# Gate and up of a SwiGLU layer: two of eight row pairs as seven block products, and x and weights asked for in order of use

## The reference

```python
h = rms_norm(x, norm_mix); proj = h @ w_in
# three head groups: gated linear attention, mLSTM, and spatial gating, whose mask is
# w_causal = tril(sgu_w)
x = x + mix @ w_out
hf = rms_norm(x, norm_ffn)
gate, up = jnp.split(hf @ w_gu, 2, axis=-1)      # w_gu: 2048 x 11264
x = x + (silu(gate) * up) @ w_down               # w_down: 5632 x 2048
return rms_norm(x, norm_final)
```

## Time and profile before

| | |
|---|---|
| median of three runs | 1117.72 us (1117.01 to 1117.94) |
| profiled execution | 1117.11 us |
| its span, first to last instruction | 1115.4 us |
| busy in the span | PE 1102.0, DVE 728.7, ACT 544.9, POOL 41.6 us |
| mean granted TensorE clock | 0.996 |
| DMA | 211.10 MB, 189 GB/s |

### The profile page before, as it was taken

How to read it: one execution, slowest core, us unless ns; L and a number is a source line. 1 busy time by engine, 2 the same in 40 slices (tenths; PEclk the granted TensorE clock), 3 DMA queues, 4 the chain that set the end, 5 groups by cost and what they waited for, 6 DMA issues and landing times.

```text
span 1115.4 us, 14031 instructions
## 1 busy us (share of the span) xinstructions
PE 1102.0 (99%) x5157; PEld 921.0 (83%) x5157; DVE 728.7 (65%) x871; ACT 544.9 (49%) x653; POOL 41.6 (4%) x66
## 2 busy tenths in 40 slices
PE   8999999999999999999999999999999999999996
PEld 7898889888888888888888888888888888888885
DVE  5456867698656555555555645555555799898895
ACT  6455545555445453444444434434444556656553
POOL 2700000000010000000000000000000000000000
PEclk9999999999999999999999999999999999999999
DMA  8665646565556666666666666666666656666663
GB/s 278 208 200 170 182 131 181 152 171 155 184 198 206 183 187 194 188 186 198 185 197 186 185 195 187 182 195 188 189 186 188 206 192 212 202 200 208 202 220 112
DMA packets 110059, 211.10 MB, mean 189 GB/s; under 512 B 6844, under 2 KB 11008, under 8 KB 109632
## 3 DMA queue, kind: packets, MB, share of 16 engines
q1 hardware_dynamic: 108960, 205.75, 60.8%
q0 software_dynamic: 1056, 4.77, 1.2%
HBM read 208.40 MB, written 2.10 MB: 189 GB/s over the span
## 4 chain that ended last, share of the span: by engine, by line
PE 96%; DVE 2%; DMA 1%; ACT 0%; issue 0%; SPq 0%; POOL 0%; ACTq 0%; POOLq 0%; DVEq 0%
PE acc L1187 24%; PE acc L1188 24%; PE acc L1189 24%; PE acc L1472 5%; PE acc L1474 5%; PE acc L1473 5%; PE mx L1179 2%; PE mx L1472 1%; PE mx L1474 1%; PE mx L1473 1%; PE mx L1358 1%; PE mx L1264 1%; DMA tok<-in_x 1%; DVE w_lo L1061 1%; DVE x L1049 0%
## 5 line engine op out<-in xcount | busy, mean ns | idle before, releaser
L658 DVE TENSOR_TENSOR w_lo<-raw,w_hi 128x1024 fp32r<-128x1024 f32 (+2 forms) x304 | 362.4, 1198 | 326.4 <-ACT w_hi L399 326.2
L399 ACT ACTIVATE w_hi<-raw 128x1024 fp32r<-128x1024 f32 (+2 forms) x304 | 314.4, 1039 | 397.3 <-PE acc L1189 387.6
L1187 PE MATMUL acc<-w_hi,hT_hi 128*128 128x512 f32 (+2 forms) x1084 | 418.5, 386 | 0.0
L1188 PE MATMUL acc<-w_lo,hT_hi 128*128 128x512 f32 (+2 forms) x1084 | 415.3, 383 | 0.0
L1189 PE MATMUL acc<-w_hi,hT_lo 128*128 128x512 f32 (+2 forms) x1084 | 415.3, 383 | 0.0
L1189 PEld LDWEIGHTS acc<-w_hi,hT_lo 128*128 128x128 f32 x1084 | 203.5, 188 | 40.1
L1187 PEld LDWEIGHTS acc<-w_hi,hT_hi 128*128 128x128 f32 x1084 | 203.6, 188 | 39.6 <-ACT tok L424 0.4
L1188 PEld LDWEIGHTS acc<-w_lo,hT_hi 128*128 128x128 f32 x1084 | 203.6, 188 | 38.7
L600 ACT ACTIVATE w_hi<-raw 128x1024 fp32r<-128x1024 f32 x88 | 83.2, 969 | 34.3 <-PE acc L1474 17.9
L1061 DVE TENSOR_TENSOR w_lo<-raw,w_hi 128x1024 fp32r<-128x1024 f32 x88 | 94.5, 1111 | 7.8 <-ACT w_hi L600 5.7
L1474 PE MATMUL acc<-w_hi,actT_lo 128*128 128x512 f32 x250 | 97.3, 389 | 0.0
(11 more groups left out here) (245 smaller groups left out, 828.4 us busy)
## 6 DMA issues: line engine op xcount, KB each, us to landing
raw<-in_w_gu SPq DMA_DIRECT2D x176, 512.0 KB, 3.7
raw<-in_w_down SPq DMA_DIRECT2D x88, 512.0 KB, 4.4
raw<-in_w_in SPq DMA_DIRECT2D x80, 512.0 KB, 4.0
raw<-in_w_out SPq DMA_DIRECT2D x32, 512.0 KB, 4.0
raw<-in_w_in SPq DMA_DIRECT2D x8, 272.0 KB, 2.8
raw<-in_w_in SPq DMA_DIRECT2D x8, 264.0 KB, 2.8
tok<-in_x SPq DMA_DIRECT2D x8, 256.0 KB, 7.4
x<-in_x POOLq DMA_DIRECT2D x2, 1024.0 KB, 9.3
```

The lines of the kernel that those rows point to most:

```text
L399: act.activation(w_hi[:, slot, 0:UC * width], raw[:, slot, 0:UC * width], ACT.Copy)\
L658: dve.tensor_tensor(w_lo[:, slot, 0:UC * width], raw[:, slot, 0:UC * width], w_hi[:, slot, 0:UC * width].bitcast(F32), ALU.subtract).then_ ...
L1187: pe.matmul(o, hi[:, c + i, tb], wh, start=first and i == 0, stop=False)
L1188: pe.matmul(o, hi[:, c + i, tb], wl, start=False, stop=False)
```

## The change

Groups 1 to 10 of gate and up take row pairs 0 and 1 as sevens: the 2 x 2 weight block is here (row block) by (gate, up), so the loads for these pairs bring the gate and the up weights of the same rows. A group has 16 loads and 20 slots in a new order `FF_ORDER`: gate 2, gate 3, seven 0, gate 4, gate 5, seven 1, gate 6, gate 7, up 2 to up 7. Group 0 stays as it was (`first_gate_up`), and makes the sums of the normed x that the sevens need (`ff_summands`). The bank sums are folded in each group (`fold_up`, `fold_gate`, `activate_folded`). The transposes of `act_tok` now stand behind the group's first unit, since the sevens use the `mx` banks.

The sums and summands lie where `x1` lies. So `x1` is stored to device memory once it is complete and loaded back when gate and up are done; DVE waits for the store in `ff_summands` and for the load in `fold_banks`.

At the start the DMAs are issued as x quarter 0, units 0 and 1, quarter 1, units 2 and 3, quarters 2 and 3, unit 4. Two x steps go ahead of the first unit, the others one by one behind units 0 to 5; each is followed by the weights of one unit on ACT and DVE. Four warm matmuls are added ahead of the x transposes and five behind the first two steps. The squares of x move from behind units 5 and 6 to behind units 8 and 9.

```diff
+FF_ORDER = [("gate", 2, 0, 0), ("gate", 3, 1, 1), ("seven", 0, 2, 2), ("gate", 4, 4, 6), ("gate", 5, 5, 7),
+            ("seven", 1, 6, 8), ("gate", 6, 8, 12), ("gate", 7, 9, 13)] + [("up", k, 8 + k, 12 + k) for k in range(2, UPG)]
+FF_SLOTS = 20
+FF_BASE = U_FF + 2 * UPG - FF_SLOTS
+FF_SLOT_OF = [-4, -3, -2, -1] + [v + d for kind, _k, _i, v in FF_ORDER for d in ((0, 1) if kind == "seven" else (0,))]
+V_DN = FF_BASE + FF_SLOTS * NG_FF
...
-WARM = 8
+WARM, WARM_X, WARM_W = 8, 4, 5
+X_AHEAD = {0: (0,), 2: (1,), 4: (2, 3)}
 LAST = 3
-START_UNITS = [0, 1, 4, 5]
...
-            for q in range(4):
-                for b in range(NB):
-                    sp.dma_start(xin[:, b, q * GW:(q + 1) * GW],
-                                 x[b * P:(b + 1) * P, q * GW:(q + 1) * GW]).then_inc(sem(f"x_loaded{b}{q}"), 16)
-                c0, width, _at = IN_GROUPS[0]
-                load(w_in, q, q, q * UC * P, c0, width, first=True)
-            for u in range(R, U_OUT):
+            for u in range(U_OUT):
+                for q in X_AHEAD.get(u, ()):
+                    for b in range(NB):
+                        sp.dma_start(xin[:, b, q * GW:(q + 1) * GW],
+                                     x[b * P:(b + 1) * P, q * GW:(q + 1) * GW]).then_inc(sem(f"x_loaded{b}{q}"), 16)
                 c0, width, _at = IN_GROUPS[u // UPG]
-                load(w_in, u, u % R, (u % UPG) * UC * P, c0, width)
+                load(w_in, u, u % R, (u % UPG) * UC * P, c0, width, first=u < R)
...
+            def load_ff(j, k, i, up):
+                sp.wait_ge(lo_ready, j * FF_SLOTS + (FF_BASE + FF_SLOT_OF[i] + 1))
+                sp.dma_start(raw[:, i % R, :].rearrange("p (k n) -> p k n", k=UC),
+                             weights(w_gu, k * UC * P, j * GW + (FF if up else 0), GW)).then_inc(loaded[i % R], 16)
+
+            for j in range(1, NG_FF):
+                for kind, k, i, _v in FF_ORDER:
+                    if kind == "seven":
+                        load_ff(j, k, i, False)
+                        load_ff(j, k, i + 1, True)
+                    else:
+                        load_ff(j, k, i, kind == "up")
 
...
+            pool.wait_ge(sem("residual_added"), 2 * NG_OUT)
+            for b in range(NB):
+                pool.dma_start(x1_kept[b * P:(b + 1) * P, :], x1[:, b, :]).then_inc(sem("x1_stored"), 16)
+
+            pool.wait_ge(unit_used, V_DN)
+            pool.wait_ge(sem("gate_used"), 2 * NG_FF)
+            pool.wait_ge(sem("x1_stored"), 16 * NB)
+            for b in range(NB):
+                pool.dma_start(x1[:, b, :], x1_kept[b * P:(b + 1) * P, :]).then_inc(sem("x1_back"), 16)
...
-                if b in START_UNITS:
-                    k = START_UNITS.index(b)
-                    high(k, k, GW, 16, fresh=True)
-
-            for u in range(R, U_FF):
+                high(b, b % R, GW, 16 * (b // R + 1), fresh=b < R)
+
+            for u in range(UPG, U_FF):
                 g = u // UPG
                 high(u, u % R, IN_GROUPS[g][1] if g < NG_IN else GW, 16 * (u // R + 1))
                 if u % UPG == 3 and 1 <= g <= NG_IN:
                     evacuate(g - 1)
-                if u in (5, 6):
-                    b = u - 5
+                if u in (8, 9):
+                    b = u - 8
...
+            def gate_up(j):
+                for kind, k, i, v in FF_ORDER:
+                    if kind == "up" and k == 3:
+                        act.wait_ge(unit_used, j * FF_SLOTS + (FF_BASE + 12))
+                        act.activation(ff_sum[:, 0, 0, :], mx[:, 2, :], ACT.Copy).then_inc(sem("p1_kept"), 1)
+                    ff_high(j, i, v)
+                    if kind == "seven":
+                        ff_high(j, i + 1, v + 1, GW)
+                        ff_sum_high(j, 0, v + 2, 2 * k + 1)
+                        if k == 0:
+                            act_high(j, j * 4 - 4)
+                        ff_sum_high(j, 1, v + 3, 2 * k + 2)
+                    if kind == "up" and k == 5:
+                        act.wait_ge(sem("gate_folded"), j * 2)
+                        gate_tanh(j * FF_SLOTS + (FF_BASE + 14), j * 2)
+
+            first_gate_up()
             with act.Fori(1, NG_FF) as j:
-                gate_up(j, False)
+                gate_up(j)
 
...
+            def activate_folded(groups, used):
+
+                for b in range(NB):
+                    if b == 0:
+                        dve.wait_ge(sem("up_block0"), groups)
+                        dve.wait_ge(sem("up_folded"), groups * 2)
+                    else:
+                        dve.wait_ge(unit_used, used)
+                    dve.tensor_tensor(up_part(b), acc[:, 2 + b, :], up_part(b), ALU.add).then_inc(sem("up_whole"), 1)
+                    if b == 0:
+                        dve.wait_ge(sem("gate_used"), groups * 2 + 2)
+                        dve.wait_ge(sem("actT_psum"), groups)
+                    dve.wait_ge(sem("up_whole"), groups * 2 + (b - 1))
+                    dve.scalar_tensor_tensor(out=act_tok[:, b, :], in0=up_part(b), scalar=half_rs2_h[:, b:b + 1],
+                                             in1=gate_s[:, b, :], op0=ALU.mult, op1=ALU.mult)\
+                       .then_inc(sem("act_ready"), 1)
+
...
+            def ff_weight_sums(j, i, k, opening=False):
+
+                a = i % R
+                for slot in range(2):
+                    dve.wait_ge(loaded[a + slot], j * (16 * 2 * UPG // R) + 16 * ((U_FF + i) // R + 1))
+                if k == 1:
+                    dve.wait_ge(lo_ready, j * FF_SLOTS + (FF_BASE + 6))
+                elif opening:
+                    dve.wait_ge(sem("ff_lo_ready"), 1)
+                else:
+                    dve.wait_ge(sem("gate_folded"), j * 2 - 2)
+                dve.tensor_tensor(ff_sum[:, 0, :, :], raw[:, a + 1, :].rearrange("p (k n) -> p k n", k=UC),
+                                  raw[:, a:a + 2, 0:GW], ALU.subtract).then_inc(sem("ff_w_sums"), 1)
+                dve.wait_ge(sem("ff_w_sums"), j * 4 + (2 * k - 3))
+                dve.tensor_tensor(ff_sum[:, 1, 0, :], raw[:, a + 1, GW:2 * GW], ff_sum[:, 0, 0, :], ALU.subtract)\
+                   .then_inc(sem("ff_t2"), 1)
+                dve.wait_ge(sem("ff_t2"), j * 2 + (k - 1))
+                dve.tensor_tensor(ff_sum[:, 1, 1, :], raw[:, a, GW:2 * GW], ff_sum[:, 1, 0, :], ALU.subtract)\
+                   .then_inc(sem("ff_w_sums"), 1)
+
+            p1, t6, t7 = (ff_sum[:, i // 2, i % 2, :] for i in range(3))
+
+            def fold_up(j):
+
+                dve.wait_ge(unit_used, j * FF_SLOTS + (FF_BASE + 12))
+                dve.wait_ge(sem("p1_kept"), j)
+                dve.tensor_tensor(t6, mx[:, 3, :], p1, ALU.add).then_inc(sem("t6_made"), 1)
+                dve.wait_ge(sem("t6_made"), j)
+                dve.tensor_tensor(t7, mx[:, 1, :], t6, ALU.add).then_inc(sem("t7_made"), 1)
+                dve.wait_ge(sem("act_ready"), j * 2)
+                dve.tensor_tensor(up_part(0), mx[:, 0, :], t6, ALU.add).then_inc(sem("up_folded"), 1)
+                dve.wait_ge(sem("t7_made"), j)
+                dve.tensor_tensor(up_part(1), mx[:, 0, :], t7, ALU.add).then_inc(sem("up_folded"), 1)
+
+            def fold_gate(j):
+
+                dve.wait_ge(unit_used, j * FF_SLOTS + (FF_BASE + 14))
+                dve.tensor_tensor(acc[:, 0, :], acc[:, 0, :], p1, ALU.add).then_inc(sem("gate_folded"), 1)
+                dve.tensor_tensor(acc[:, 1, :], acc[:, 1, :], t7, ALU.add).then_inc(sem("gate_folded"), 1)
+
...
+            def gate_up(j, opening=False, summed=True):
+                for kind, k, i, v in FF_ORDER:
+                    if kind == "seven":
+                        ff_weight_sums(j, i, k, opening)
+                    ff_low(j, i, v)
+                    if kind == "seven":
+                        if k == 0:
+                            if opening:
+                                activate(FF_SLOTS + FF_BASE, 2)
+                            else:
+                                activate_folded(j - 1, j * FF_SLOTS + FF_BASE)
+                        ff_low(j, i + 1, v + 1, GW)
+                        ff_sum_low(j, 0, v + 2)
+                        if k == 0:
+                            act_low(j, j * 4 - 4, summed)
+                            if summed:
+                                act_sums(j, bass.ds(j - 1, 1))
+                        ff_sum_low(j, 1, v + 3)
+                    if kind == "up":
+                        if k == 2:
+                            fold_up(j)
+                        if k == 5:
+                            fold_gate(j)
+                        if k == 6:
+                            gated(j * 2)
+
...
+                dve.wait_ge(sem("x1_back"), 16 * NB)
...
+            keep_warm(WARM)
             pe.wait_ge(sem("norm_loaded"), 16)
             transpose(acc[:, 2, 0:KC], rowsN, KC).then_inc(sem("colsT_psum"), 1)
-            for b in range(4):
-                x_transposed(b)
+            keep_warm(WARM_X)
+            x_transposed(0)
```

(75 more changed lines are left out.)

154 lines of the change are left out of this document (102 added, 52 removed).

## The result

The changed kernel takes 1119.87 us in the median of seven runs (1117.46 to 1122.5), the kernel before 1117.27 us (1116.73 to 1117.94) beside it: ratio 1.0021, 95% interval 1.0012 to 1.0031. The medians are 2.6 us apart, about 2.4 us by the ratio: the kernel is slower. I had forecast 1116.8 us, no change.

What follows compares the result with a forecast made beforehand. TensorE was taken as the bound, with 96% of the chain that ended last. Terms of -13.6 (matmuls), +11.6 (group waits) and +1.7 us (start) gave -0.3 us on 1117.1, so 1116.8 us; range 1107 to 1123.

Steps and rivals of the forecast that it cites:

- the multiplications: Gate and up, groups 1 to 10: six fewer matmuls per group, 60 in all at 0.2267 us, 13.6 us off.
- the nine waits: Groups 2 to 10: TensorE waits 1.29 us for `activate_folded` before the transposes behind the first unit, 11.6 us in all.
- The walk through VectorE's queue: Gate and up, around a group's first unit: VectorE's instructions timed in order, `activate_folded` ending at 3.9 us, TensorE wanting it at 2.72.
- the lower bound of 1.04 us: Group wait if the weight load lands at once and VectorE's own queue decides: 1.04 us each, 9.4 us in all.
- "no second wait" at v4: Gate and up, behind the transposes: low parts and sums ready at t + 4.0 us, TensorE asks at t + 4.76.
- everything in the walk is counted from the group's own boundary, so it comes back each time: Groups 2 to 10: the same 1.29 us wait recurs in all nine groups, 11.6 us on.
- the clock's fall: Rival, chance 0.12: clock drops to 1.2 GHz, 1.6 us lost; behind unit 15 1118.4 us, in each of nine groups 1131.
- a rival for late loads: Gate and up, load for weight pair i=3 lands late: slower by 2.2 us at about 4.1 us, 1123 at 4.4; chance 0.13.
- estimate of 3.3 us for the load: Gate-and-up weight load from about 2.0 us fixed cost plus bytes: sum 2.3 us lower; not used, the trace's 3.7 us was.
- GpSimd late, +2.8 us: Start, transposes behind unit 15: GpSimd's mask done at 60.3 us, TensorE waits 2.8 us, 1.7 us later than before.
- the rival at 0.10: Start: GpSimd is in time, so TensorE does not wait for its mask; 1114 us, chance 0.10.
- nothing in the down stage: Start of the down stage: `activate_folded` ends 1.0 us later than `activate`, costing nothing, at most 1 us.

Runs made afterwards that it cites:

- two moves: Changed kernel with `activate_folded` ahead of the `low` of v2 in every group and `gated` behind the `low` of up 7 instead of up 6: 1104.02 us, ratio 0.9878.
- the experiment that shortened group 2's wait alone: Changed kernel with group 2 written out on TensorE and VectorE (1120.88 us), plus `activate_folded` ahead of the `low` of v2 in group 2 only: 1117.84 us.
- the second execution: Changed kernel, no edit, the second of two more profiled executions: 1121.64 us, clock falls at groups 2 and 4.
- the start-only kernel: Kernel before with only the change's new start (load order, warm matmuls, x steps, squares), gate and up as before: 1117.22 us, ratio 0.9998.
- gate and up alone: Changed kernel with the start of the kernel before, so only the sevens and the kept residual are new: 1117.8 us, ratio 1.0005.
- with the old start: Changed kernel with later `gated` and earlier `activate_folded`, but loads, warm matmuls and first copies ordered as in the kernel before: 1105.04 us, ratio 0.9887.
- `gated` later: Changed kernel with `gated` behind the `low` of up 7 instead of up 6, nothing else moved: 1113.92 us, ratio 0.9969.

## Why the prediction was wrong

**Right: the multiplications.** A group without waits is 1.25 to 1.34 us shorter than before, of the forecast 1.36 us; the term of -13.6 us holds but for the small gaps.

**Right in place and mechanism, a little small: the nine waits.** Forecast 1.29 us each and 11.6 us in all; 13.0 us in the profile, since the load took 3.96 us in the mean and not 3.7. The walk through VectorE's queue, the lower bound of 1.04 us and "no second wait" at v4 held, and two moves chosen by that walk removed the wait. What it left out was about 1.0 us of small gaps, 0.1 us in a group.

**Wrong: "everything in the walk is counted from the group's own boundary, so it comes back each time".** This is the step that failed, and with it the clock's fall, a rival that the sum put at nothing. The load's time is not counted from the boundary: at group 2 it was 5.0 us, not 3.7, and the wait 2.3 us. I had a rival for late loads and one for the clock, and kept them apart; in fact the falls come behind the waits that a late load made long. By their times 14 of the 20 runs had one or two falls, each worth 1.6 to 1.7 us in the rows; that is the larger part of what the median has above the fastest execution. It is shown by the executions without a fall and with two, and by the experiment that shortened group 2's wait alone: 3.0 us off, and no mean clock under 0.997. My argument against the clock's fall, that a wait of 1.3 us is short, held for waits of that size: no profile here has a fall behind a gap under 2.2 us in this stage. Of the longer ones, 2.29 us (group 4 of the second execution), 2.41, 2.78 and 2.85 us (group 2) had one; 2.31, 2.71 and 2.75 us had none. A fall accounts for 1.7 of the 2.5 us between two heaps of runs; the rest is not accounted for.

The page "TensorE: Matmul & The Clock Gate" of the Trainium skill, Part 1, says that the idle array drops to 1.2 GHz. The rows above agree in that the four falls begin in a gap of 2.29 us or more, or at most 1.4 us behind its end; here such a wait brings one in some executions and not in others.

The estimate of 3.3 us for the load, worked out from the Trainium skill's page "DMA: Bandwidth & Descriptors", would have made the sum 2.3 us lower. That page gives its 2.0 us for DMAs on GpSimd's path, and these loads are SP's. The nine took 3.62 to 5.00 us: it was right not to use it.

**Wrong: GpSimd late, +2.8 us.** The squares ended at 36.65, not 37.5, and GpSimd's chain took 20.7 us (36.84 to 57.53), not 22.8. TensorE waited about nothing. The start was -1.0 us and not +1.7; the rival at 0.10 was true. Alone this error would have put the forecast 2.7 us too high.

**Wrong: nothing in the down stage.** It took 0.8 us more, and in the start-only kernel 1.2 us more, most of it in each a single wait behind VectorE; in gate and up alone it took 0.1 us more. So it came with the new start rather than with the sevens. The residual's way out and back cost nothing that shows.

The terms that were off by -2.7, +1.4, +1.0 and +0.8 us cancelled nearly, so by luck the profiled execution came out as forecast, +0.3 against -0.3 us. The median has the falls as well.

## What to carry to other kernels

Walk the queue of the engine that feeds a moved step, and use the same walk to choose the order: here two moves of a few lines, an activation ahead of a `low` that nobody waits for and a gating behind one that frees a buffer, turned +2.6 into -13.2 us (-12.2 us with the old start). A wait of 1.3 us that comes nine times is dearer than its sum, for it leaves no slack for one late load, and here one that made a gap of 2.3 us or more took the clock with it in some executions. When a kernel's runs lie in heaps, look at profiles from several heaps before explaining the median, and add a change's halves before trusting either: here -0.1 and +0.5 made +2.6, and with the two moves the start's share could not be told from the noise.

## What the hardware showed unexpectedly

Warm matmuls of 32 columns in f32 took as long as those of 128. Each is two rows of the trace: 13.86 us for 32 of them (64 rows) and 3.52 us for eight (16 rows) are both 0.22 us a row. Each row has a weight load of 128x128 beside it, and these were busy for 13.7 of the 13.9 us. The same load of 512 KB, issued at the same place of the same queue, took 3.8 us or 5.0 us depending on an edit 460 us earlier. With the waits shortened the runs drew together: a spread of 5.6 us in eleven runs of the changed kernel, 2.0 us in six with `gated` later, 1.4 us in four with both moves.
